# Merging and routing three of five token tiles beneath the expert slots of the other two

## The reference

```
for l in range(2):
    sh1, sc1, g1, sh2, sc2, g2 = split(silu(cond) @ w_mod + b_mod, 6)
    h = rmsnorm(x) * (1 + sc1) + sh1
    cq, ckv, krope, zb, qc, kc, vc, gates = split(h @ w_in)      # three branches and their gates
    merged = sum(sigmoid(gates[b]) * (branch[b] @ w_o[b]) for b in range(3))
    x = x + g1 * (merged @ w_out)
    h = rmsnorm(x) * (1 + sc2) + sh2
    q = h @ w_pq                                    # 8 heads x 2 x 128
    top 16 of 128 scores on both sides, top 16 of their 256 sums   # 8 heads x 16 = 128 slots a token
    x = x + g2 * sum over slots of gate * gelu(u_tab[e] . h) * v_tab[e]
```

## Time and profile before

| | |
|---|---|
| runs | 5893.99, 5882.26, 5882.52 us, median 5882.52 |
| span of the profiled execution | 5888.0 us (its own time is not listed apart from these runs) |
| TensorE busy | 4851.9 us, 82% |
| VectorE, ScalarE, POOL busy | 3117.5, 1068.8, 1547.3 us |
| moved by DMA | 1509.10 MB, 1344.88 of it by gathers |
| granted clock of TensorE | 0.957 of full, mean |

### The profile page before, as it was taken

How to read it: one execution, slowest core, us unless ns; L and a number is a source line. 1 busy time by engine, 2 the same in 40 slices (tenths; PEclk the granted TensorE clock), 3 DMA queues, 4 the chain that set the end, 5 groups by cost and what they waited for, 6 DMA issues and landing times.

```text
span 5888.0 us, 54180 instructions
## 1 busy us (share of the span) xinstructions
PE 4851.9 (82%) x13846; PEld 2304.7 (39%) x13846; DVE 3117.5 (53%) x7277; ACT 1068.8 (18%) x2738; POOL 1547.3 (26%) x1465
## 2 busy tenths in 40 slices
PE   9999999967777777777799999999777777777776
PEld 3578544522222222222235784445222222222222
DVE  2454112176676677676625541122666676676775
ACT  0223100122111211211102220011221121211211
POOL 0200000034334334443302000000333443434443
PEclk9989999999999999999999999999999999999999
DMA  6110111199999999999861002112999999999998
GB/s 260 49 37 1 75 50 72 67 382 372 379 372 368 387 377 386 393 374 381 346 247 57 20 1 75 65 65 100 383 371 388 359 378 379 379 377 387 376 378 338
DMA packets 213890, 1509.10 MB, mean 256 GB/s; under 512 B 24652, under 2 KB 26316, under 8 KB 33996
## 3 DMA queue, kind: packets, MB, share of 16 engines
q0 software_dynamic: 185040, 1344.88, 58.0%
q1 hardware_dynamic: 20880, 141.57, 6.2%
q10 hardware_dynamic: 7800, 20.57, 1.0%
HBM read 1503.65 MB, written 3.28 MB: 256 GB/s over the span
## 4 chain that ended last, share of the span: by engine, by line
PE 44%; DMA 22%; DVE 20%; issue 7%; DVEq 3%; POOL 2%; ACT 1%; ACTq 0%; POOLq 0%
DMA arena<-in_experts,arena 21%; PE ps L473 12%; DVE sq L1299 11%; PE ps L697 7%; PE ps L664 4%; PE ps L645 3%; PE ps L594 3%; PE ps L622 2%; PE ps L656 2%; POOL arena L442 2%; PE ps L493 2%; DVE arena L1202 2%; PE ps L606 2%; DVE arena L1205 1%; DVE arena L1203 1%
## 5 line engine op out<-in xcount | busy, mean ns | idle before, releaser
L697 PE MATMUL ps<-arena 128*128 128x512 f32 x5120 | 2539.0, 645 | 972.0 <-ACT arena L888 934.3
L1299 DVE CUSTOM_DVE_ANT_0 sq<-arena,z 128x1024 f32<-128x1024 f32 x1280 | 1569.8, 1226 | 1024.3 <-DMA arena<-in_experts,arena 957.8
L442 POOL DMA_INDIRECT arena<-in_experts,arena x1280 | 1418.6, 1108 | 2408.2 <-PE ps L697 1980.5
L697 PEld LDWEIGHTS ps<-arena 128*128 128x128 f32 x5120 | 995.3, 203 | 2514.8 <-ACT arena L888 1398.3
L473 PE MATMUL ps<-arena 128*128 128x512 f32 (+3 forms) x1920 | 757.8, 551 | 0.0
L881 ACT ACTIVATE arena<-arena 128x2 f32<-128x2 f32 x640 | 130.1, 204 | 2704.3 <-DVE arena L1299 2704.3
L426 POOL TENSOR_SCALAR ss<-ss 128x1 f32<-128x1 f32 (+3 forms) x86 | 29.7, 345 | 1846.7 <-DVE ss L961 1328.5
L473 PEld LDWEIGHTS ps<-arena 128*128 128x128 f32 x1920 | 364.2, 191 | 370.4 <-issue 336.7
L888 ACT ACTIVATE arena<-ident,arena 128x128 f32<-128x128 f32 x1280 | 439.5, 393 | 128.3 <-DVE arena L1309 127.7
L664 PE MATMUL ps<-arena 128*128 128x128 f32 (+1 forms) x992 | 268.2, 429 | 2.5 <-ACTq L745 2.5
L1119 DVE TENSOR_REDUCE negm<-ps 128x1 f32<-128x768 f32 (+4 forms) x160 | 118.9, 744 | 264.7 <-PE ps L601 164.0
(11 more groups left out here) (166 smaller groups left out, 3447.3 us busy)
## 6 DMA issues: line engine op xcount, KB each, us to landing
arena<-in_weights SPq DMA_DIRECT2D x122, 1024.0 KB, 6.8
arena<-in_experts,arena POOLq DMA_INDIRECT x1280
big<-mod_rows ACTq DMA_DIRECT2D x16, 512.0 KB, 8.6
arena<-in_weights SPq DMA_DIRECT2D x8, 576.0 KB, 4.5
arena<-in_weights SPq DMA_DIRECT2D x4, 768.0 KB, 4.7
arena<-in_weights SPq DMA_DIRECT2D x6, 512.0 KB, 4.2
big<-in_g_norm ACTq DMA_DIRECT2D x4, 512.0 KB, 12.4
x<-in_x_sample POOLq DMA_DIRECT2D x4, 512.0 KB, 5.9
```

What stands on the lines that cost most here:

```text
L442: pool.indirect_dma_start(out=ring[s % RING], out_offset=None, in_=ins["experts"], in_offset=bass.IndirectOffsetOnAxis(ap=ihead[:, s:s + 1 ...
L697: last = MM(a[:, c * 512:(c + 1) * 512], diag[s % RING], ring[s % RING][:, D + c * 512:D + (c + 1) * 512], start=False, stop=False)
L1299: last = V.tensor_tensor_reduce(out=sq[:], in0=ring[r][:, 0:D], in1=h2[:, i, :], scale=1.0, scalar=0.0, op0=ALU.mult, op1=ALU.add, accum_o ...
```

## The change

The four engine programs and SP now walk one common list of items for both layers, `ITEMS`, made by `schedule()`; no hardware loops are left.

- **Order.** Tiles 0 and 1 (`GROUPS[0]`) are merged, projected and routed first. Their slots then begin, pair by pair, and `Spread.stretch` lays the remaining work between the pairs by a table of costs: six pairs under the last queries of group 0, 104 pairs with the merge and routing of tiles 2 to 4 and the choice of tile 1, 12 with the choice of tile 2, 8 with nothing. Under tile 3 of layer 0 lies the modulation of layer 1.
- **A pair** consists of `E` (two dot products; ScalarE's square, scaled copy and two tanh; multiplication by the gates), `Ewt` of the pair before (weights, diagonals) and `Emm` of the pair before that (sums).
- **Sums on 64x64 tiles.** The diagonal tile is cut into its two halves of 64, and a pair becomes 8 matmuls of 64 x 64 by 512 columns on the four quarters of the array. Even slots add into the half of PSUM where the token lies, odd slots into the other half; the odd sum is swapped back once a tile (`ex`, `sw`, `ew`).
- **Buffers.** The first 16 slots of tile 0 use four gather buffers, the rest of tiles 0 and 1 five, tiles 2 to 4 eight; the other three lie where hT of tiles 2 and 3, the merged rows and the gates are until routing is over. The four diagonal tiles replace eight. Weight buffers go from five to three, and the blocks of merge, output and queries are loaded once for each group.
- **Engines.** Gelu and sigmoid are made from tanh; the transposed probabilities are copied by ScalarE; the root of the second norm is computed by VectorE with 12 small operations in place of POOL's power; all top-16 of single scores (`tk1`) come right after the scores; all transfers except gathers go through SP.

```diff
-NU = 5
...
-RING = 8
 GRP = 2
-BODY = 32
...
+NU = 3
...
+def turn(l, t, u):
+    return [("tk2", l, t, u), ("tkx", l, t, u), ("tkg", l, t, u)]
...
+def merge(l, gid):
+    tiles = GROUPS[gid]
+    s = []
     for bc in range(6):
-        for i in range(NT):
-            s += [("g", bc, i), ("p", bc, i)]
-    s += [("mT", 0)]
-    for i in range(NT):
-        s += [("o", i, 0)] + ([("mT", i + 1)] if i + 1 < NT else []) + [("o", i, 1)]
-        s += [("hT", 1, i - 1)] if i else []
-    s += [("hT", 1, NT - 1)]
-    for q in range(16):
-        s += [("pq", q)]
-        s += [("sc", q - 1)] if q else []
-    s += [("sc", 15)]
+        for t in tiles:
+            s += [("g", l, bc, t), ("p", l, bc, t)]
+    s += [("mT", l, tiles[0])]
+    for j, t in enumerate(tiles):
+        s += ([("mT", l, tiles[j + 1])] if j + 1 < len(tiles) else []) + [("o", l, t, 0)]
+    for j, t in enumerate(tiles):
+        s += [("o", l, t, 1), ("n2", l, t)]
+        s += [("hT2", l, tiles[j - 1])] if j else []
+    return s + [("hT2", l, tiles[-1])]
...
+def route(l, gid, early=None):
+
+    s = []
+    for q in range(17):
+        s += [("pq", l, gid, q)] if q < 16 else []
+        if q:
+            s += [("sc", l, gid, q - 1), ("tk1", l, gid, q - 1)]
+        if q and q % 4 == 0 and early is not None:
+            s += turn(l, early, q // 4 - 1)
...
+GROUPS = {0: (0, 1), 1: (2, 3, 4)}
...
+    def group(self):
+        if self.later:
+            self.items += self.later.pop(0)
+        self.items.append(("E", self.dotted))
+        self.dotted += 1
+        if self.dotted - self.weighted > 1:
+            self.weigh()
+        if self.weighted - self.added > 1:
+            self.add()
...
+def schedule():
+    s = Spread()
+    s.items += [("start",), ("consts", 0)] + mod_items(0)
+    for l in range(L):
+        s.items += norm_and_inputs(l) + attention(l) + merge(l, 0)
+        r = route(l, 0, 0)
+        at = r.index(("pq", l, 0, 6))
+        s.items += r[:at]
+        s.stretch(r[at:], 6)
+        s.stretch(choose(l, 1) + merge(l, 1) + route(l, 1), 2 * NGRP - SEAM - 12 - 6)
+        s.stretch(choose(l, 2), 12)
+        s.stretch([], SEAM + 2)
+        s.stretch(choose(l, 3), 16)
+        beneath = [("consts", 1)] + mod_items(1) if l == 0 else []
+        s.stretch(beneath, NGRP - 16)
+        s.stretch(choose(l, 4), 16)
+        s.stretch([], 2 * NGRP - 18)
+        s.flush()
+    return s.items
...
+NBUF = 8
+BUF = []
+for _l, _t in ETILES:
+    BUF += [(s % 4 if _t == 0 and s < 16 else (s + 4) % 5 if _t == 0 else (s + 2) % 5 if _t == 1 else s % NBUF) for s in range(SLOTS)]
...
+                        if slot % 32 == 0:
+                            pool.wait_ge(*ready("tk2", l, t, slot // 32))
+                        if SAME[n] is not None:
+                            pool.wait_ge(slot_used, SAME[n] + 1)
+                        if n == FIRST_IN[l, BUF[n]] and BUF[n] == 4:
+                            pool.wait_ge(*full("pq", l, GROUP_OF[1], 15))
+                        if n == FIRST_IN[l, BUF[n]] and BUF[n] in (5, 6, 7):
+                            pool.wait_ge(*full("pq", l, LAST_GROUP, 15))
+                        pool.indirect_dma_start(
+                            out=ring[BUF[n]], out_offset=None, in_=ins["experts"],
+                            in_offset=bass.IndirectOffsetOnAxis(ap=index[n // SLOTS % 2][:, slot:slot + 1], axis=0)
+                        ).then_inc(row_land[BUF[n]], 16)
...
+                elif kind == "Emm":
+                    n = GRP * item[1]
+                    e, s = divmod(n, SLOTS)
+                    if s == 0 and e % NT:
+                        pe.wait_ge(acc_free, e)
+                        pe.wait_ge(*ready("ex", *ETILES[e - 1]))
+                    elif s == 0:
+                        for before in ACC_BEFORE[item[1]]:
+                            pe.wait_ge(*ready(*before))
+                    for odd in range(2):
+                        pe.wait_ge(row_land[BUF[n + odd]], 16 * TURN_OF[n + odd])
+                    pe.wait_ge(diag_done, n + 2)
                     for c in range(2):
-                        MM(a[:, c * 512:(c + 1) * 512], zeros[:], h2[:, i, c * 512:(c + 1) * 512], start=True, stop=False)
-                    with pe.Fori(0, TURNS) as t:
-                        for s in range(BODY):
-                            pe.wait_ge(diag_ready.sem, l * diag_ready.layer + t * BODY + (i * SLOTS + s + 1))
-                            for c in range(2):
-                                last = MM(a[:, c * 512:(c + 1) * 512], diag[s % RING], ring[s % RING][:, D + c * 512:D + (c + 1) * 512], start=False, stop=False)
-                            last.then_inc(slot_used.sem, 1)
-                    for c in range(2):
-                        last = MM(a[:, c * 512:(c + 1) * 512], zeros[:], h2[:, i, c * 512:(c + 1) * 512], start=False, stop=True)
-                    last.then_inc(acc_full.sem, 1)
-                pe.drain().then_inc(layer_end.sem, 1)
-                pe.wait_ge(layer_end.sem, layer_end.at(l, 5))
-
+                        for odd in range(2):
+                            for h in range(2):
+                                lo, to = 64 * h, 64 * (h ^ odd)
+                                last = MM(acc[h][to:to + 64, c * 512:(c + 1) * 512], diag[(n + odd) % 4][lo:lo + 64, lo:lo + 64],
+                                          ring[BUF[n + odd]][lo:lo + 64, D + c * 512:D + (c + 1) * 512], start=s == 0, stop=s == SLOTS - 2)
+                    last.then_inc(slot_used, 2)
...
+                elif kind == "ex":
+                    t = item[2]
+                    e = l * NT + t
+                    act.wait_ge(slot_used, SLOTS * (e + 1))
+                    if e:
+                        act.wait_ge(*full("sw", *ETILES[e - 1], 1))
+                    A(cross[0:64, :], acc[1][0:64, :], ACT.Copy)
+                    out(A(cross[64:128, :], acc[0][64:128, :], ACT.Copy))
+                elif kind == "E":
+                    n = GRP * item[1]
+                    c = n % 8
+                    act.wait_ge(dot_done, n + GRP)
+                    A(dsq[:, c:c + GRP], dots[:, c:c + GRP], ACT.Square, scale=(GELU_A * GELU_B) ** 0.5)
+                    A(dlin[:, c:c + GRP], dots[:, c:c + GRP], ACT.Copy, scale=GELU_A)
+                    act.drain()
+                    for s in range(c, c + GRP):
+                        last = A(dth[:, s:s + 1], dsq[:, s:s + 1], ACT.Tanh, scale=dots[:, s:s + 1], bias=dlin[:, s:s + 1])
+                    last.then_inc(tanh_done, 1)
+                elif kind == "Ewt":
+                    act.wait_ge(wts_done, item[1] + 1)
+                    for n in (GRP * item[1], GRP * item[1] + 1):
+                        if n >= 4:
+                            act.wait_ge(slot_used, n - 3)
+                        A(diag[n % 4], ident[:], ACT.Copy, scale=wts[:, n % 8:n % 8 + 1]).then_inc(diag_done, 1)
...
+                elif kind == "E":
+                    n0 = GRP * item[1]
+                    c = n0 % 8
+                    for n in range(n0, n0 + GRP):
+                        dve.wait_ge(row_land[BUF[n]], 16 * TURN_OF[n])
+                        V.tensor_tensor_reduce(out=sq[:], in0=ring[BUF[n]][:, 0:D], in1=h2_of_slot(n), scale=1.0, scalar=0.0,
+                                               op0=ALU.mult, op1=ALU.add, accum_out=dots[:, n % 8:n % 8 + 1]).then_inc(dot_done, 1)
+                        dve.drain()
+                    s = n0 % SLOTS
+                    TT(dgate[:, c:c + GRP], dots[:, c:c + GRP], gate[n0 // SLOTS % 2][:, s:s + GRP], ALU.mult)
+                    dve.drain()
+                elif kind == "Ewt":
+                    c = GRP * item[1] % 8
+                    dve.wait_ge(tanh_done, item[1] + 1)
+                    STT(wts[:, c:c + GRP], dth[:, c:c + GRP], 1.0, dgate[:, c:c + GRP], ALU.add, ALU.mult).then_inc(wts_done, 1)
```

More of the change, by code:

```diff
@@ new lines, in blocks_of @@
+def blocks_of(item):
+    k = item[0]
+    l = item[1] if len(item) > 1 else None
+    if k == "mod":
+        return [(l, -1, ("mod", item[2], h)) for h in range(2)]
+    if k in ("kv", "cq", "u", "v", "qc", "kc"):
+        return [(l, 0, (k, 0, h)) for h in range(2)]
+    if k == "ukv":
+        return [(l, 0, ("ukv", 0, 0))]
+    if k == "uq":
+        return [(l, 0, ("uq", 0, item[3]))]
+    if k == "vm":
+        return [(l, 0, ("ws", 0, 0))]
+    if k == "g":
+        return [(l, GROUP_OF[item[3]], ("gate", item[2], h)) for h in range(2)]
+    if k == "p":
+        return [(l, GROUP_OF[item[3]], ("proj", item[2], 0))]
+    if k == "o":
+        return [(l, GROUP_OF[item[2]], ("out", item[3], h)) for h in range(2)]
+    if k == "pq":
+        return [(l, item[2], ("pq", item[3] // 2, 0))]
+    return []
@@ new lines @@
+LOADS = []
+LOAD_NO = {}
+FINAL_ITEM = {}
+for _it in ITEMS:
+    for _b in blocks_of(_it):
+        if _b not in LOAD_NO:
+            LOAD_NO[_b] = len(LOADS)
+            LOADS.append(_b)
+        FINAL_ITEM[_b] = _it
```

(28 more changed lines are left out.)

1966 lines of the change are left out of this document (963 added, 1003 removed).

## The result

The changed kernel takes **7554.97 us** (median of four runs, 7551.17 to 7575.87) where the kernel before takes 5888.26 beside it: a ratio of 1.284, 95% interval 1.280 to 1.287. It is slower, inside the range, 225 us above the forecast of 7330. The profiled execution has a span of 7553.1 us.

What follows compares the result with a forecast made beforehand. TensorE bounds the dense stages; in the slot stage the DMA limit and the eight-buffer round are nearly equal. Layer 0 at 3747 and layer 1 at 3587 make 7334, less 5: 7330 us, range 6650 to 8050.

Steps and rivals of the forecast that it cites:

- The buffers: In tiles 0 and 1, five buffers make sum, gather, landing and dots a closed round of one pair: 13.4 us, against 5.52.
- The sum on 64x64 tiles: TensorE's 16 quarter-size records a pair in the slot stage: taken as 3.7 us, between 1.9 and 7.1.
- the second of the two reasons given for 3.7: In a pair's sum, four array parts work together at half clock, because the gaps are over 3 us.
- rival (b): In the sums, all four array parts work together at full clock: round 11.6 us, total 6890 us; chance 0.26.
- The merge beneath: Merge and routing of three tiles under 104 pairs, 327 us of TensorE a layer, 3.1 us a pair: hidden, cost nothing.
- The dense stages: Before the pairs: modulation 145 us (33 in layer 1), inputs and attention 522, merge of two tiles 173, queries 35.
- First ten pairs: Start of the slots: first six pairs, under the rest of the queries, 90 us; later pairs of tiles 0 and 1 13.4 each.
- Tiles 2 to 4: 192 pairs a layer with eight buffers at 5.6 us a pair: 1075 us, plus 60 for layer 0's modulation.
- The modulation beneath: The next layer's modulation under tile 3 of layer 0: 24 weight blocks, 25 MB, cost 60 us in a DMA-filled stage.
- the choice of tables: On VectorE beneath the pairs: four choices of 11 us, 44 in all, hidden; tiles 2 to 4 kept 5.6 us a pair.
- the round of eight buffers: In tiles 2 to 4: 13.4 plus 2.5 for the second gather, 15.9 us over three pairs, 5.3 a pair.
- The gain: Work moved out of the dense stages to beneath the slots: 2 x 327 us, and 70 of modulation.

Runs made afterwards that it cites:

- e2: The changed kernel with five gather buffers in tiles 2 to 4 too, where no merge lies beneath; 10004.8 us (a single run).
- e4: The kernel before with four gather buffers instead of eight and nothing else changed; 11938.5 us (a single run).
- e6: The changed kernel with six buffers instead of five under tiles 0 and 1 from slot 16 on, and gates before projections in the merge; 6640.07 us.
- e9: The changed kernel with weights and diagonals of a pair directly behind its own dot products, its sum left behind the following merge item; 6065.35 us.
- e1: The changed kernel with weights and sum of a pair directly after its own dot products instead of one and two pairs later; 6696.94 us.
- e5: The kernel before with weights and diagonals of a pair directly behind its own dot products instead of the next pair's; 5635.92 us, ratio 0.9585.
- e8: The kernel of e6 with, from tile 2 on, weights and sum directly behind a pair's own dot products; 6264.77 us.
- e7: The changed kernel with sums on whole 128x128 tiles, 8 matmul records a pair in place of 16 quarter ones; 8215.29 us.

## Why the prediction came out

**The buffers: right**, in cause and size. Five buffers close a ring of one pair: e2 (with no merge beneath) shows it and e4 (four buffers, with nothing of the change) bears it out, e6 loosens it by one buffer, e9 by one position in the queue. Term by term, from the chain above: release to landing 0.26 + 5.48 where I had 0.80 + 5.7; dot 1.23 as said; from it to the diagonals 1.07 against 0.44 + 0.8; diagonals 0.59 (0.69); to TensorE 0.14 (0.05); sum 3.73 (3.7). The sum of it is 12.5 and not 13.4; the largest error is in the first two terms: the 0.80 ahead of a gather is 0.26 in the chains of the changed kernel, and the landing is 0.2 shorter. The prediction priced the unrolled loops at nothing; that this 0.5 us is theirs is likely, but no run separates it. Over 118 pairs a layer and with the choices, tiles 0 and 1 took 1506 us from slot 20 on where my terms give 1593.

**The sum on 64x64 tiles: right, by the second of the two reasons given for 3.7.** All four parts of the array do work together: 16 records in 1.95 us, which is what the Trainium skill says of different tiles ("TensorEngine Tiling (Array Packing)", Key Properties); the trace agrees. And at the lower clock they take 3.69. So rival (b) had the array right and the clock wrong. Which of the two a pair gets goes with what TensorE did before: beneath the merge it was 1.92 or 1.95 directly behind merge items, and 3.69 in 48 of the 54 sums that came after a gap of over 5 us. The mean there is 3.12 (312.4 us busy for 100 pairs), not 3.7; the warm sums stand behind merge items, where their shortness makes up for the item.

**The merge beneath: right.** 12.64 us a pair with it, 12.54 and 12.79 with nothing. It was hidden because the ring left room; where the ring is shorter that room is gone: 10.66 against 6.6 in e1, 8.06 against 6.5 in e9.

**The dense stages: right.** First gather at 882 us where my sum gave 875; layer 1's 786 us after the end of the slots of layer 0 (3840 to 4626 us), where the terms 33, 522, 173 and 35 give 763. The change adds 30 weight loads a layer, as forecast (200 in place of 140 for both layers; so the kernel before loads 70 blocks a layer, not 56).

**First ten pairs: too low.** 90 + 4 x 13.4 = 144 forecast, 187 and 184 measured. The 90 was put together from VectorE's work and rounds of four buffers; which of its terms was too small was not separated.

**Tiles 2 to 4: the step that failed.** I gave them 5.6 us a pair, 1075 us a layer, 1135 with the modulation. They took 1265 and 1211, 6.6 and 6.3 a pair. That is 265 us more than forecast, more than the 225 by which the whole was low; the shorter ring of tiles 0 and 1 gave 173 back (2 x 87), the first ten pairs took 83. So the total is as near as it is because errors of both signs met. The modulation beneath was priced well: 44 pairs at 6.98 against 5.70 are 56 us, forecast 60.

The term that failed most is the choice of tables, which the 5.6 took over from the kernel before ("now 5.52 with the choices"). The changed kernel makes each choice as one block on VectorE, four in 16 pairs, where the kernel before spread it over a turn in pieces (`choose_keys(turn, part)`). The block itself had been priced right, at 11 us; its first and last instruction (3079.87 to 3091.38) are 11.5 apart:

```profile
3079.87 0.69 DVE L1333 TENSOR_TENSOR arena<-arena 128x512 f32<-128x512 f32 x1
...
3091.20 0.18 DVE L1356 TENSOR_SCALAR arena<-arena 128x32 uint32<-128x32 f32 x1
```

But in tiles 2 to 4 it was put at nothing. A block stands ahead of the dot products of a pair, and behind it sum, gather and landing follow in turn; four pairs then take 33 us. The 38 pairs a layer in slots 256 to 296 and 384 to 420 took 8.4 to 8.5 us on average in place of 5.6, which is 217 of the 265 us. The kernel before had 5.5 there, and e5, with prompt weights and pieces, 5.2, where e8 and e9, with prompt weights and blocks, have 6.7 to 7.9. So the blocks cost with either order; no run spreads them in the changed kernel, and up to that this cause is read from the stretches.

The other 48 us are in the pairs without choices, at 5.7 to 5.8 us. There the round of eight buffers was too short: "13.4 + 2.5 for the second gather", 15.9 over three pairs. It has a lone landing in it, but with eight buffers several rows are in flight at once and a landing takes longer (at 10.3 us a landing and a gather every 2.9 us, three to four; that is an estimate from these rows). The trace before had said so: 8.73 us in the earlier trace rows. The changed kernel's chain has it at 10.3 to 11.5:

```profile
3607.80 1.98 PE ps L920 x16
3609.78 0.26 issue
3610.04 1.00 POOL arena L682
3611.04 0.30 issue
3611.35 10.30 DMA arena<-in_experts,arena
...
3621.67 1.23 DVE sq L1374
...
3624.69 1.98 PE ps L920 x16
```

That is 16.9 us from sum to sum (3607.80 to 3624.69), 5.6 a pair, and the share of DMA is 0.94 and not 1. That the lag costs this, and not the clock, e8 and e9 show: with prompt weights and granted clocks of 0.74 and 0.77 there (0.74 in the changed kernel) the last tile has 5.07 to 5.11, the DMA limit.

**The gain** was there, if smaller than the 724 us forecast (2 x 327 and 70): 221 us ahead of the first gather of layer 0, and 324 between the gathers of the two layers (4032 - 2919 before, 4626 - 3837 now), where the modulation went too. The forecast counted the slots of the kernel before from 1171 us on, but its first gather starts at 1103, still under the routing. It was never the merge's cost that was in question but what space the merge keeps: three of eight buffers, for 128 of 320 pairs.

## What to carry to other kernels

Count, for a ring of buffers, how many units of work lie between freeing a buffer and the event that frees the next of the same place: buffers minus what the software pipeline holds back. One stage of lag too many costs a landing in each turn, and where buffers are just enough it costs even with nothing else changed (here 4.2% of the kernel before, by moving the weights and diagonals of a pair ahead). With that order the round has room, and only then is it worth asking what lies beneath. Before work is laid beneath a DMA-bound stage, ask which memory it keeps from that stage; do not take the price of a piece of work from a kernel that spreads it, when the new one does it in one block; and give each engine's queue the order in which the long operation stands ahead of the one that waits.

## What the runs showed of the hardware

A sum of 64x64 tiles can run at half clock after gaps after which a sum of the whole array did not. In the kernel before, eight 128x128 records took 3.70 us after a gap of 1.25, in e7 3.67 after 2.07. In the changed kernel 16 quarter records took 3.69, not 1.95, after 1.99 and 1.27:

```profile
3299.78 3.69 PE L920 MATMUL ps<-arena 64*64 64x512 f32 x16 [1.99 <-ACT arena L1061]
3304.74 3.69 PE L920 MATMUL ps<-arena 64*64 64x512 f32 x16 [1.27 <-ACT arena L1061]
```

The granted clock in these two sums is 0.50 (1.2 GHz). It is not so after every such gap: of the 49 sums that the timeline lists by themselves in tiles 2 to 4 of layer 0 after gaps of 1.2 to 2.1 us, 32 ran at full clock, 11 at half and 6 in between. In e7, with sums of the whole array, all 16 such sums of these tiles ran at full clock, and in the slot stage of the kernel before 128 of 129. So a part of what was saved on the array is lost on the clock. Still a cold quarter sum (3.69) takes as long as a warm one of the whole array (3.70), and e7 shows that on balance the quarters gain 660 us, with a mean granted clock of 0.762 against 0.822. What decides between the two levels after equal gaps these runs don't settle.

The second surprise is e4: halving the buffers of a kernel with a DMA share of 0.96 doubles its time (11938.5, a single run, against 5888). At eight buffers the ring, 15.39 us over three pairs, and the channel (5.2 a pair) were equal to within 2%, and in the page's slices only the full channel shows.
